# Three ordinary column pairs in place of four in each feed-forward of a one-core transformer step

## The chip, the cores and the metric

The kernel runs on one core of one Trainium2 chip. The metric is the device time of one execution in microseconds (us); the time of a version is the median of its runs. Engines are named as in the profile: PE is TensorE's matmul stream and PEld its weight loads, DVE is VectorE, ACT is ScalarE, POOL is GpSimd, and SP is the sync engine, which here only issues the DMAs of the large inputs. `L805` is line 805 of the kernel's file.

## What is computed

One layer of a hybrid backbone on 640 tokens (128 context and 512 latent) of width 1024, all in float32: a half-step SwiGLU feed-forward, a token mixer, and a second half-step feed-forward, each with RMS norms and with shift, scale and gate vectors from a modulation product. What matters here are the two feed-forwards and the modulation:

```python
def swiglu(h, w_in, w_out):
    g, u = jnp.split(h @ w_in, 2, axis=-1)
    return (jax.nn.silu(g) * u) @ w_out

mod = (jax.nn.silu(cond) @ w_mod + b_mod)[:, None, :]
sh1, sc1, g1, sh2, sc2, g2, sh3, sc3, g3 = jnp.split(mod, 9, axis=-1)
h = rms_norm(x, norm_pre[0]) * (1.0 + sc1) + sh1
x = x + 0.5 * g1 * rms_norm(swiglu(h, ffn_w_in[0], ffn_w_out[0]), norm_post[0])
```

`ffn_w_in` has 2 x 2816 columns, which are 22 pairs of a gate block and a value block of 128 columns each; `w_mod` has 9 x 1024 columns, loaded as 18 slabs of 512 columns (2 MB each).

## The kernel before, in words

**Precision.** Each float32 operand is split into a high and a low part of the fast matmul type, and a product is three matmuls: high by high, high by low, low by high. For a weight slab (1024 rows x 128 columns, 512 KB) SP loads the whole into the buffer of the low part (`load`, L411), ACT casts the high part (`next_hi`, L1198), POOL subtracts to get the low part (`subtract`, L534, and `low`, L544), and PE multiplies. Some slabs of later stages are subtracted by DVE (`LO_DVE`, L137).

**Stages.** `STAGES` (L48) lists the weight slabs of every stage with the ring of buffers through which they go, and `plan` (L85) works out from it which slab must be done before a buffer is loaded again (`FREE`). `FRESH` (L106) is the order in which ACT and POOL prepare ordinary slabs. The stages are `in0`, `in0s` (first feed-forward, input side), `out0A`, `out0B` (its output side, for the token tiles 0 to 2 and then 3 and 4), the mixer from `vuA` to `woB`, and `in1A`, `in1B`, `in1s`, `out1A`, `out1B`. In `in1A` and `in1B` the same ordinary slabs are used twice, for tokens 0 to 383 and for the rest, and stay in their buffers.

**Two kinds of column pair.** The first `EARLY_PAIRS` = 4 pairs of each feed-forward are ordinary: 2 slabs x 8 row blocks x 3 passes over all 640 tokens, 96 matmuls of 320 columns or as many columns in another cut. The other `SEVEN` = 18 pairs use a seven-product scheme on 2 x 2 quadrants (`seven_products`, L816): 7 products x 4 row blocks x 3 passes = 84 matmuls of 320 columns (`product`, L801). It needs combinations of the weights, made for each pair (`first_sums` L1910, `last_sum` L1926 and `lows` L1937 on DVE; `gate_highs` L1418 and `value_highs` L1424 on ACT; `seven_low` L552 on POOL), and combinations of the tokens, made once for a feed-forward (`token_combinations` L1892 on DVE, `token_highs` L1439 on ACT, `token_lows` L547 on POOL). Each product waits for its operands; the second product of the first pair also waits until the hidden tiles of the ordinary pairs have left PSUM (L833).

**Order in the first feed-forward.** After each ordinary slab named in `MOD_AFTER` (slabs 2, 3, 5 and 7) and after each of the first ten seven-product pairs, PE multiplies one modulation slab (`late_mod`, L874). SP's list (L459 to L486) puts the loads in one queue: slabs 4, 5 and 6, modulation slab 2, slab 7, and then for each seven-product pair its two slabs and one more modulation slab. A modulation slab waits until the one before it has been used (`next_mod`, L469). On DVE the weight sums and lows of the first seven-product pair come behind the hidden tile of ordinary pair 2 (L2032); on ACT its casts come in ordinary pairs 2 and 3 (L1486 to L1489).

**The output side.** `out_group` on PE (L723) runs 22 slabs for three token tiles in `out0A` (11 slabs for the first 512 output columns, 11 for the rest). Slab m of the first 11 needs hidden tiles 0 to 2m+1, split into high and low:

```python
            if grp == 0 and blk == 0:
                pe.wait_ge(sem(ready[0]), ready[1] + k + 2)
```

ACT makes the cast (`whole_high`, L1326) and DVE the subtraction (`whole_low`, L1963). The first `EARLY_PAIRS` + 2 casts come before the stage. The others are spread over it, two behind each slab and behind the weight casts that `after_slab` (L1205) releases there:

```python
                after_slab(i + m, 2 if grp else 1)
                ...
                    for j in range(EARLY_PAIRS + 2 * m + 2, min(FT, EARLY_PAIRS + 2 * m + 4)):
                        whole_high(b // 2, j)
```

SP loads slab m+4 when slab m is done, and puts the two DMAs of the gain rows ahead of slab 8 (`load_gains`, L436).

Of the kernel before, what the change touches and what calls it, by code (L numbers as in the profile page):

```python
# [26 lines left out]

GROUP = ((0, 1, 2), (3, 4))
G_COLS = ((0, 384), (384, 640))
EARLY_PAIRS = 4  # L30

# [4 lines left out]
SEVEN = FT - EARLY_PAIRS  # L38
# [7 lines left out]

KEEP = [6, 7, 8, 9, 10]
STAGES = [  # L48
    ("in0", 2 * EARLY_PAIRS, [0, 1, 2, 11, 0, 1, 2, 0], False),
    ("in0s", 2 * SEVEN, [12, 1, 2, 0], False),  # L50
    ("out0A", FT, [1, 2, 0, 3], False), ("out0B", FT, [0, 4, 5, 1, 2], False),
    ("vuA", 8, [6, 1, 7, 2, 8, 0, 9, 10], False), ("vuB", 8, [6, 1, 7, 2, 8, 0, 9, 10], True),
    ("heads", 4 * NH, [1, 2, 0], False),
    ("merge", 3 * KT, [2, 0, 1], False),
    ("woA", KT, KEEP[:3] + [2, 0, 1] + KEEP[3:], False),
    ("woB", KT, KEEP[:3] + [2, 0, 1] + KEEP[3:], True),
    ("in1A", 2 * EARLY_PAIRS, KEEP[:2] + [2, 0, 1] + KEEP[2:], False),
    ("in1B", 2 * EARLY_PAIRS, KEEP[:2] + [2, 0, 1] + KEEP[2:], True),
    ("in1s", 2 * SEVEN, [12, 2, 0, 1], False),
    ("out1A", FT, [2, 0, 1, 3], False), ("out1B", FT, [1, 4, 5, 2, 0], False),  # L60
]


MOD_ROUNDS = ((0, 2), (1, 3))
MOD_AFTER = [2, 3, 5, 7]
EARLY_GATES = 3
LAST = 3

# [16 lines left out]
def plan():  # L85
# [35 lines left out]
    branch = base["merge"] + MERGE.index(("br", 3))  # L121
    for n, after in ((0, branch), (1, branch), (2, branch), (6, base["woA"] - 1), (7, base["woA"] - 1)):
        free[base["woA"] + n] = after
    for n, after in ((0, base["woA"]), (1, base["woA"] + 1)) + tuple((n, base["in1A"] - 1) for n in (5, 6, 7)):
        free[base["in1A"] + n] = after
    free[base["in0s"]] = 4
    free[base["in1s"]] = base["in1A"] - 1
    return base, buf, free, order, need, fresh


def hybrid_step_kernel(nc, x_prompt, x_sample, state_hgrn, c, c_ctx, w_mod, b_mod, norm_pre, norm_post,
# [53 lines left out]
    def tile_at(n):  # L185
        return mid_at + n * TB
# [213 lines left out]
    def _(sp):  # L400
# [70 lines left out]
            sp.wait_ge(sem("mod_mm"), MOD_EARLY + (1 if i == 2 else i))  # L471
            load_mod(i)

        for n in (4, 5, 6):
            load_in0(n)
        next_mod(2)
        load_in0(7)
        for p in range(SEVEN):
            j = EARLY_PAIRS + p
            load(BASE["in0s"] + 2 * p, 0, KT, w0[:, :, j * P:(j + 1) * P])  # L480
            load(BASE["in0s"] + 2 * p + 1, 0, KT, w0[:, :, DFF + j * P:DFF + (j + 1) * P])
            if 3 + p < MOD_LATE:
                next_mod(3 + p)
        wo0 = ffn_w_out[0, 0].rearrange("(k p) n -> p k n", p=P)
        load_out(0, 0, wo0)
        load_out(0, 1, wo0)  # L486
# [46 lines left out]
    def _(pool):  # L533
# [35 lines left out]
        for n, i in enumerate(FRESH):  # L569
            if n < 3 or i in LO_DVE:  # L570
                continue
            if i in (6, BASE["out1A"]):
                token_lows(int(i != 6))
            if i in (BASE["out0A"], BASE["out1A"]):
                for p in range(SEVEN):
                    seven_low(int(i == BASE["out1A"]), p)
            step = 2 if BASE["heads"] <= i < BASE["merge"] + 2 * EARLY_GATES else 4
            pool.wait_ge(hi_done, n + 1)
            for k in range(0, KT, step):
                m = subtract(i, k, k + step)  # L580
            m.then_inc(lo_done, 1)
# [611 lines left out]
    def _(act):  # L1193
# [287 lines left out]
        for j in range(EARLY_PAIRS):  # L1481
            after_slab(2 * j)
            gate_out(j, (two(TT[0][:, :]), halves(2 if j == 1 else 0)))
            if j == 1:
                token_highs(0)
            if j == 2:  # L1486
                gate_highs(0, 0)
            if j == 3:
                value_highs(0, 0)  # L1489
            after_slab(2 * j + 1)  # L1490
        seven_gates(0)
# [181 lines left out]
        for stage, grp in (("in1A", 0), ("in1B", 1)):  # L1673
            c0, c1 = G_COLS[grp]
            for j in range(EARLY_PAIRS):
                n = (1 + grp) * EARLY_PAIRS + j
                after_slab(BASE[stage] + 2 * j)
                gate_out(n, (TT[0][:, c0:c1], bank(early_bank(grp, j, 0))[:, 0:c1 - c0]))
                if (grp, j) == (0, 0):
                    h_high_half(1, 4)  # L1680
                    h_hi(1, 4)
                if (grp, j) == (1, 0):
                    token_highs(1)
                if (grp, j) == (1, 1):
                    gate_highs(1, 0)
                if (grp, j) == (1, 2):
                    value_highs(1, 0)
        seven_gates(1)
        out_group(2, 0)
# [3 lines left out]
    def _(dve):  # L1693
# [332 lines left out]
        for j in range(EARLY_PAIRS):  # L2026
# [2 lines left out]
            V.tensor_tensor(two(M32[:, j, :]), two(TT[0][:, :]), halves(1), ALU.mult).then_inc(sem("hid_ready"), 1)  # L2029
            if j == 0:  # L2030
                token_combinations(0)
            if j == 2:  # L2032
                first_sums(0, 0)
                last_sum(0, 0)
                lows(0, 0)
# [327 lines left out]
```

## Time and profile before

| | us |
|---|---|
| runs | 1403.70, 1403.95, 1404.72 |
| median of the 3 runs | 1403.95 |
| the profiled execution's own time | 1403.82 |
| its span, first to last instruction | 1401.9 |
| PE busy in the span | 1380.4 (98%) |
| mean granted TensorE clock | 0.999 of full speed |

A timeline row gives the start in us from the span's start, the length in us, the engine, the line, the operation with output and inputs, the count of merged instructions, and in brackets the idle time before it with what ended it. Matmuls overlap in the pipeline: a matmul of 320 columns is shown with some 0.31 us, but the next one starts 0.147 us later. So lengths of PE work are taken from start to start. A DVE or POOL row begins when the engine takes the instruction up, so a row can hold a wait for a resource.

### The profile page before, as it was taken

The numbers are of one execution on the slowest core, as the hardware profiler recorded it, in microseconds if no ns is written. First come the engines' busy times: TensorE is split into PE (matmuls) and PEld (weight loads), VectorE is DVE, ScalarE is ACT, GpSimd is POOL, SyncE is SP. The second block draws the span as 40 slices with busy tenths as digits, with TensorE's granted clock in tenths as the row PEclk, the third lists the DMA queues.
The fourth block names the chain that finished last, engine by engine and source line by source line (L and its number), as shares of the span: only waits on it lengthen the run. The fifth ranks groups of instructions, "written<-read, shape, count | busy, mean of one in ns | idle before, by whom it ended". The sixth has DMA issues, their size and how long they took to land.

```text
span 1401.9 us, 23454 instructions
## 1 busy us (share of the span) xinstructions
PE 1380.4 (98%) x9561; PEld 1261.6 (90%) x9561; DVE 722.6 (52%) x1086; ACT 578.3 (41%) x933; POOL 716.1 (51%) x528
## 2 busy tenths in 40 slices
PE   6999999999999999999999999999999999999998
PEld 5799898999888888999999999988999999988886
DVE  5726565766712431478776312235567666676033
ACT  5233333444534663244445222257243443355243
POOL 1465545465865672324223433542466655668653
PEclk9999999999999999999999999999999999999999
DMA  9756676233535651212112222333122223334465
GB/s 347 258 156 221 216 234 210 61 92 90 173 127 166 194 174 49 61 54 62 53 41 65 76 76 76 106 105 105 32 75 84 81 78 91 91 104 153 135 195 181
DMA packets 215294, 173.34 MB, mean 124 GB/s; under 512 B 6472, under 2 KB 175636, under 8 KB 215060
## 3 DMA queue, kind: packets, MB, share of 16 engines
q1 hardware_dynamic: 212448, 170.61, 39.1%
q8 instruction: 76, 1.25, 0.4%
q10 hardware_dynamic: 2740, 1.24, 0.3%
q14 instruction: 30, 0.25, 0.1%
HBM read 168.65 MB, written 3.17 MB: 123 GB/s over the span
## 4 chain that ended last, share of the span: by engine, by line
PE 91%; DVE 2%; ACT 2%; DMA 1%; issue 1%; POOL 1%; SPq 1%; ACTq 0%; DVEq 0%; POOLq 0%
PE PP L805 31%; PE PP L603 27%; PE PP L622 9%; PE PP L624 9%; PE PP L623 9%; PE PP L661 2%; DMA W_in<-in_ffn_w_in 1%; PE PP L869 1%; PE PP L995 1%; PE PP L647 1%; POOL W_lo L536 1%; PE PP L1011 1%; DVE XTOK L1796 0%; ACT W_hi L1203 0%; ACT YB L1280 0%
## 5 line engine op out<-in xcount | busy, mean ns | idle before, releaser
L536 POOL TENSOR_TENSOR W_lo<-W_in,W_hi 128x512 fp32r<-128x512 f32 (+1 forms) x308 | 386.3, 1280 | 448.2 <-ACT W_hi L1203 440.8
L545 POOL TENSOR_TENSOR W_lo<-W_in,W_hi 128x512 fp32r<-128x512 f32 x108 | 169.6, 1584 | 190.4 <-ACT S_hi L1430 186.3
L1203 ACT ACTIVATE W_hi<-W_in 128x1024 fp32r<-128x1024 f32 x145 | 153.0, 1056 | 220.6 <-PE PP L624 116.3
L622 PE MATMUL PP<-W_hi,Mlo 128*128 128x512 f32 x440 | 172.5, 392 | 2.3 <-POOL W_lo L536 1.9
L624 PE MATMUL PP<-W_hi,Mhi 128*128 128x512 f32 x440 | 171.3, 389 | 0.0
L623 PE MATMUL PP<-W_lo,Mlo 128*128 128x512 f32 x440 | 171.3, 389 | 0.0
L603 PE MATMUL PP<-Hhi,W_hi 128*128 128x320 f32 (+2 forms) x640 | 154.1, 316 | 0.0
L603 PE MATMUL PP<-Hlo,W_hi 128*128 128x320 f32 (+2 forms) x640 | 149.6, 309 | 0.0
L603 PE MATMUL PP<-Hhi,W_lo 128*128 128x320 f32 (+2 forms) x640 | 149.6, 309 | 0.0
L805 PE MATMUL PP<-Hhi,W_hi 128*128 128x320 f32 x432 | 134.9, 312 | 0.5 <-DVE TT L1989 0.5
L805 PE MATMUL PP<-Hhi,W_lo 128*128 128x320 f32 x432 | 133.5, 309 | 0.0
L805 PE MATMUL PP<-Hlo,W_hi 128*128 128x320 f32 x432 | 133.4, 309 | 0.0
L603 PEld LDWEIGHTS PP<-Hhi,W_hi 128*128 128x128 f32 x640 | 106.6, 188 | 4.7 <-issue 3.5
L545 POOL TENSOR_TENSOR S_lo<-S_in,S_hi 128x512 fp32r<-128x512 f32 x72 | 108.1, 1502 | 3.4 <-ACT S_hi L1431 3.4
L603 PEld LDWEIGHTS PP<-Hlo,W_hi 128*128 128x128 f32 x640 | 108.1, 188 | 0.0
L603 PEld LDWEIGHTS PP<-Hhi,W_lo 128*128 128x128 f32 x640 | 108.0, 188 | 0.0
L622 PEld LDWEIGHTS PP<-W_hi,Mlo 128*128 128x128 f32 x440 | 82.6, 188 | 22.0 <-issue 2.3
L624 PEld LDWEIGHTS PP<-W_hi,Mhi 128*128 128x128 f32 x440 | 82.6, 188 | 17.4
L623 PEld LDWEIGHTS PP<-W_lo,Mlo 128*128 128x128 f32 x440 | 82.6, 188 | 16.9
L805 PEld LDWEIGHTS PP<-Hhi,W_hi 128*128 128x128 f32 x432 | 81.1, 188 | 10.0 <-issue 9.1
L805 PE MATMUL PP<-T_hi,S_hi 128*128 128x320 f32 x288 | 89.0, 309 | 0.0
L805 PE MATMUL PP<-T_lo,S_hi 128*128 128x320 f32 x288 | 89.0, 309 | 0.0
(280 smaller groups left out, 2966.3 us busy)
## 6 DMA issues: line engine op xcount, KB each, us to landing
W_in<-in_ffn_w_out SPq DMA_DIRECT2D x176, 256.0 KB, 3.3
W_in<-in_ffn_w_in SPq DMA_DIRECT2D x83, 512.0 KB, 4.5
modl<-in_w_mod SPq DMA_DIRECT2D x14, 2048.0 KB, 8.1
W_in<-in_w_in SPq DMA_DIRECT2D x32, 512.0 KB, 3.8
modw<-in_w_mod SPq DMA_DIRECT2D x4, 2048.0 KB, 14.1
HL<-g_rows SPq DMA_DIRECT2D x6, 512.0 KB, 6.2
V_in<-in_w_in SPq DMA_DIRECT2D x10, 256.0 KB, 4.1
O_in<-in_w_out SPq DMA_DIRECT2D x10, 256.0 KB, 6.2
```

Of the source, the lines that this page charges most:

```text
L536: return nc.gpsimd.tensor_tensor(lo[:, k0:k1, :], full[:, k0:k1, :], hi[:, k0:k1, :].bitcast(fp32), ALU.subtract)
L545: return nc.gpsimd.tensor_tensor(lo, full, hi.bitcast(fp32), ALU.subtract)
L603: m = mm(out[:, 0:c1 - c0], w[:, k, :], src[:, c0:c1], start=lead and n == 0 and a == 0, stop=tail and n == len(x) - 1 and a == 2)
L622: mm(out, xh, wh, start=lead and kk == 0, stop=False)
L623: mm(out, xh, wl, start=False, stop=False)
L624: m = mm(out, xl, wh, start=False, stop=tail and kk == 1)
L647: return nc.tensor.transpose(out, in_, ident[0:k, 0:k])
L661: m = mm(PP[3][32 * q:32 * q + 32, 0, :], S2[:, k, 30 - 2 * i:62 - 2 * i], w[:, k, :], start=first and k < 4, stop=k >= 4, skip_group_chec ...
L805: m = mm(out, wk[:, k, :], xk[:, k, :], start=not add and k == 0 and a == 0, stop=k == KH - 1 and a == 2, skip_group_check=add)
L869: m = mm(PP[n][:, half, 0:HALF], w[:, k, :], src[:, half * HALF:(half + 1) * HALF], start=k == 0 and a == 0, stop=k == KT - 1 and a == 2)
L995: m = mm(near(pair_of(hd, lev))[32 * q:32 * q + 32, ch, :], KX[lev % 2][:, at:at + 32], queries, start=True, stop=True)
L1203: A(W[i][0], W[i][2], ACT.Copy).then_inc(hi_done, 1)
```

## The change

`EARLY_PAIRS` becomes 3, so that each feed-forward has 3 ordinary and 19 seven-product pairs, and what depends on it is moved:

- Slabs 6 and 7 of `in0` and the last two of `in1A` and `in1B` are dropped. `MOD_AFTER` becomes slabs 2, 3 and 5, so modulation slab 3 is multiplied behind the first seven-product pair.
- SP: the value slab of the first seven-product pair is loaded behind modulation slab 2. Then SP waits until modulation slab 1 has been used and loads its gate slab. From then on a pair's two slabs come ahead of the modulation slab that used to come one pair earlier.
- DVE: the weight sums and lows of the first seven-product pair move from behind ordinary pair 2 to behind pair 1. In the second feed-forward `token_combinations` moves ahead of the hidden tile of pair 2, and the weight sums move behind the first hidden tile of `in1B`.
- ACT: `value_highs` of the first seven-product pair directly follows `gate_highs`. POOL: in the first feed-forward `token_lows` now follows all ordinary slabs.
- Buffers 0, 1 and 2 are renamed in all later stages. In `in1s` the first pair gets the buffers 12 and 9, which are free as soon as `in1A` begins.

```diff
-EARLY_PAIRS = 4
+EARLY_PAIRS = 3
...
-    ("in0", 2 * EARLY_PAIRS, [0, 1, 2, 11, 0, 1, 2, 0], False),
-    ("in0s", 2 * SEVEN, [12, 1, 2, 0], False),
-    ("out0A", FT, [1, 2, 0, 3], False), ("out0B", FT, [0, 4, 5, 1, 2], False),
+    ("in0", 2 * EARLY_PAIRS, [0, 1, 2, 11, 0, 1], False),
+    ("in0s", 2 * SEVEN, [12, 2, 0, 1], False),
+    ("out0A", FT, [0, 1, 2, 3], False), ("out0B", FT, [2, 4, 5, 0, 1], False),
...
-    ("in1A", 2 * EARLY_PAIRS, KEEP[:2] + [2, 0, 1] + KEEP[2:], False),
-    ("in1B", 2 * EARLY_PAIRS, KEEP[:2] + [2, 0, 1] + KEEP[2:], True),
-    ("in1s", 2 * SEVEN, [12, 2, 0, 1], False),
-    ("out1A", FT, [2, 0, 1, 3], False), ("out1B", FT, [1, 4, 5, 2, 0], False),
+    ("in1A", 2 * EARLY_PAIRS, KEEP[:2] + [1, 2, 0] + KEEP[2:3], False),
+    ("in1B", 2 * EARLY_PAIRS, KEEP[:2] + [1, 2, 0] + KEEP[2:3], True),
+    ("in1s", 2 * SEVEN, [12, 9] + [1, 2, 0, 12] * SEVEN, False),
+    ("out1A", FT, [1, 2, 0, 3], False), ("out1B", FT, [0, 4, 5, 1, 2], False),
...
-MOD_AFTER = [2, 3, 5, 7]
+MOD_AFTER = [2, 3, 5]
...
-        for n in (4, 5, 6):
+        for n in (4, 5):
             load_in0(n)
         next_mod(2)
-        load_in0(7)
-        for p in range(SEVEN):
+        j = EARLY_PAIRS
+        load(BASE["in0s"] + 1, 0, KT, w0[:, :, DFF + j * P:DFF + (j + 1) * P])
+
+        sp.wait_ge(sem("mod_mm"), MOD_EARLY + 2)
+        load(BASE["in0s"], 0, KT, w0[:, :, j * P:(j + 1) * P])
+        for p in range(1, SEVEN):
             j = EARLY_PAIRS + p
-            load(BASE["in0s"] + 2 * p, 0, KT, w0[:, :, j * P:(j + 1) * P])
-            load(BASE["in0s"] + 2 * p + 1, 0, KT, w0[:, :, DFF + j * P:DFF + (j + 1) * P])
-            if 3 + p < MOD_LATE:
-                next_mod(3 + p)
+            load_pair(BASE["in0s"] + 2 * p, w0, j)
+            if 2 + p < MOD_LATE:
+                next_mod(2 + p)
...
             if j == 2:
                 gate_highs(0, 0)
-            if j == 3:
                 value_highs(0, 0)
...
             if j == 0:
                 token_combinations(0)
-            if j == 2:
+            if j == 1:
                 first_sums(0, 0)
                 last_sum(0, 0)
                 lows(0, 0)
...
         early_hidden(0, 1)
+        token_combinations(1)
         early_hidden(0, 2)
-        token_combinations(1)
-        early_hidden(0, 3)
         early_hidden(1, 0)
-        early_hidden(1, 1)
         first_sums(1, 0)
         last_sum(1, 0)
+        early_hidden(1, 1)
+        lows(1, 0)
         early_hidden(1, 2)
-        lows(1, 0)
-        early_hidden(1, 3)
         seven_sums(1)
```

## Rows read from the trace of the kernel before

**Rows 1.** The page, part 1: busy time of each engine over the span.
```profile
PE 1380.4 (98%) x9561; PEld 1261.6 (90%) x9561; DVE 722.6 (52%) x1086; ACT 578.3 (41%) x933; POOL 716.1 (51%) x528
```

**Rows 2.** Waits of PE: total us, times, longest us.
```profile
PE PP L622 <- POOL W_lo L536: 1.9, 3, 0.7
```

**Rows 3.** Timeline of PE, end of the ordinary pairs, first feed-forward.
```profile
83.04 1.92 PE L661 MATMUL PP<-modl,S 128*32 128x512 f32 x16
...
99.16 1.92 PE L661 MATMUL PP<-modl,S 128*32 128x512 f32 x16
101.02 0.42 PE L805 MATMUL PP<-Hhi,W_hi 128*128 128x320 f32 x1
```

**Rows 4.** Timeline of DVE: the same sum of two neighbouring seven-product pairs.
```profile
299.53 0.49 DVE L1989 TENSOR_TENSOR TT<-TT,PP 128x320 f32<-128x320 f32 x1 [3.09 <-PE PP L805]
...
311.85 0.49 DVE L1989 TENSOR_TENSOR TT<-TT,PP 128x320 f32<-128x320 f32 x1 [3.09 <-PE PP L805]
```

**Rows 5.** Timeline of PE, ordinary pairs of the second feed-forward.
```profile
966.26 0.33 PE L603 MATMUL PP<-Hhi,I_hi 128*128 128x384 f32 x1
...
974.61 1.04 PE L647 MATMUL PP<-ident,YB 128*128 128x128 f32 x8
...
1000.47 0.28 PE L603 MATMUL PP<-Hhi,I_hi 128*128 128x256 f32 x1
...
1023.50 0.31 PE L805 MATMUL PP<-Hhi,W_hi 128*128 128x320 f32 x1
```

**Rows 6.** Timeline of PE in `out0A`: slabs 0, 7 and 8 begin.
```profile
345.85 0.47 PE L622 MATMUL PP<-W_hi,Mlo 128*128 128x512 f32 x1 [0.66 <-POOL W_lo L536]
...
374.69 0.39 PE L622 MATMUL PP<-W_hi,Mlo 128*128 128x512 f32 x1
...
378.94 0.50 PE L622 MATMUL PP<-W_hi,Mlo 128*128 128x512 f32 x1
```

**Rows 7.** The page, part 6: DMAs, KB each, median us from issue to landing.
```profile
W_in<-in_ffn_w_in SPq DMA_DIRECT2D x83, 512.0 KB, 4.5
modl<-in_w_mod SPq DMA_DIRECT2D x14, 2048.0 KB, 8.1
```

**Rows 8.** Timeline of POOL: token lows and first pair's lows, first feed-forward.
```profile
72.52 8.83 POOL L545 TENSOR_TENSOR T_lo<-T_in,T_hi 128x1280 fp32r<-128x1280 f32 x3 [7.19 <-ACT T_hi L1442]
...
94.05 1.36 POOL L545 TENSOR_TENSOR S_lo<-S_in,S_hi 128x512 fp32r<-128x512 f32 x1 [3.43 <-ACT S_hi L1431]
```

**Rows 9.** Timelines of POOL and DVE in `in1B`: a DVE sum beside POOL's token lows.
```profile
1006.92 8.80 POOL L545 TENSOR_TENSOR T_lo<-T_in,T_hi 128x1280 fp32r<-128x1280 f32 x3 [15.06 <-ACT T_hi L1442]
...
1013.06 3.21 DVE L1919 TENSOR_TENSOR S_in<-W_in 128x512 f32<-128x512 f32 x1 [0.45 <-DMA W_in<-in_ffn_w_in]
1016.30 0.69 DVE L1923 TENSOR_TENSOR S_in<-S_in,W_in 128x512 f32<-128x512 f32 x1
```

**Rows 10.** Timelines of DVE and ACT: token combinations of the second feed-forward.
```profile
992.82 1.48 DVE L1890 TENSOR_TENSOR BSUM<-Hhi,Hlo 128x1280 f32<-128x1280 f32 x1
...
1003.25 1.49 DVE L1908 TENSOR_TENSOR T_in<-T_in,BSUM 128x1280 f32<-128x1280 f32 x1
...
1005.58 3.58 ACT L1442 ACTIVATE T_hi<-T_in 128x1280 fp32r<-128x1280 f32 x3
```

**Rows 11.** Timelines of SP, ACT and DVE in `out0A`.
```profile
367.83 32.17 SPq L423 DMA_DIRECT2D W_in<-in_ffn_w_out  x17
...
373.93 1.06 ACT L1203 ACTIVATE W_hi<-W_in 128x1024 fp32r<-128x1024 f32 x1 [4.37 <-DMA W_in<-in_ffn_w_out]
374.89 1.35 ACT L1335 ACTIVATE Mlo<-M 128x640 fp32r<-128x640 f32 x2
...
375.65 10.56 DVE L1965 TENSOR_TENSOR Mhi<-M,Mlo 128x640 fp32r<-128x640 f32 x6 [3.28 <-ACT Mlo L1335]
```

**Rows 12.** Timelines of PE and DVE in `out1A`.
```profile
1274.90 0.39 PE L622 MATMUL PP<-W_hi,Mlo 128*128 128x512 f32 x1
...
1274.91 10.58 DVE L1965 TENSOR_TENSOR Mhi<-M,Mlo 128x640 fp32r<-128x640 f32 x6 [1.48 <-ACT Mlo L1335]
```

More of the change, by code:

```diff
@@ L48 @@
 STAGES = [
-    ("in0", 2 * EARLY_PAIRS, [0, 1, 2, 11, 0, 1, 2, 0], False),
-    ("in0s", 2 * SEVEN, [12, 1, 2, 0], False),
-    ("out0A", FT, [1, 2, 0, 3], False), ("out0B", FT, [0, 4, 5, 1, 2], False),
[L52 to L56, printed above, removed]
-    ("in1A", 2 * EARLY_PAIRS, KEEP[:2] + [2, 0, 1] + KEEP[2:], False),
-    ("in1B", 2 * EARLY_PAIRS, KEEP[:2] + [2, 0, 1] + KEEP[2:], True),
-    ("in1s", 2 * SEVEN, [12, 2, 0, 1], False),
-    ("out1A", FT, [2, 0, 1, 3], False), ("out1B", FT, [1, 4, 5, 2, 0], False),
+    ("in0", 2 * EARLY_PAIRS, [0, 1, 2, 11, 0, 1], False),
+    ("in0s", 2 * SEVEN, [12, 2, 0, 1], False),
+    ("out0A", FT, [0, 1, 2, 3], False), ("out0B", FT, [2, 4, 5, 0, 1], False),
+    ("vuA", 8, [6, 0, 7, 1, 8, 2, 9, 10], False), ("vuB", 8, [6, 0, 7, 1, 8, 2, 9, 10], True),
+    ("heads", 4 * NH, [0, 1, 2], False),
+    ("merge", 3 * KT, [1, 2, 0], False),
+    ("woA", KT, KEEP[:3] + [1, 2, 0] + KEEP[3:], False),
+    ("woB", KT, KEEP[:3] + [1, 2, 0] + KEEP[3:], True),
+    ("in1A", 2 * EARLY_PAIRS, KEEP[:2] + [1, 2, 0] + KEEP[2:3], False),
+    ("in1B", 2 * EARLY_PAIRS, KEEP[:2] + [1, 2, 0] + KEEP[2:3], True),
+    ("in1s", 2 * SEVEN, [12, 9] + [1, 2, 0, 12] * SEVEN, False),
+    ("out1A", FT, [1, 2, 0, 3], False), ("out1B", FT, [0, 4, 5, 1, 2], False),
 ]
 MOD_ROUNDS = ((0, 2), (1, 3))
-MOD_AFTER = [2, 3, 5, 7]
+MOD_AFTER = [2, 3, 5]
 EARLY_GATES = 3
@@ L123, in plan @@
         free[base["woA"] + n] = after
-    for n, after in ((0, base["woA"]), (1, base["woA"] + 1)) + tuple((n, base["in1A"] - 1) for n in (5, 6, 7)):
+    for n, after in ((0, base["woA"]), (1, base["woA"] + 1)) + ((5, base["in1A"] - 1),):
         free[base["in1A"] + n] = after
-    free[base["in0s"]] = 4
+    free[base["in0s"]] = 3
     free[base["in1s"]] = base["in1A"] - 1
+    free[base["in1s"] + 1] = base["in1A"] - 1
     return base, buf, free, order, need, fresh
@@ L206, in hybrid_step_kernel @@
     EXTRA = slab_buffer("W11", tile_at(14) - 8192)
+    KEPT["in1s"] = KEPT["in1A"]
     KEPT.update({"vuB": KEPT["vuA"], "woB": KEPT["woA"], "in1B": KEPT["in1A"]})
@@ L571, in _ @@
                 continue
-            if i in (6, BASE["out1A"]):
-                token_lows(int(i != 6))
+            if i in (BASE["out0A"], BASE["out1A"]):
+                token_lows(int(i == BASE["out1A"]))
             if i in (BASE["out0A"], BASE["out1A"]):
@@ L1685, in _ @@
                     gate_highs(1, 0)
-                if (grp, j) == (1, 2):
                     value_highs(1, 0)
```

## The prediction

> **What bounds the kernel now.** I read the page's busy line first, then the waits of PE, then timelines. The busy line shows PE at 1380.4 of 1401.9 us [rows 1]: PE is the bound from its first matmul to the end. The waits show why PE work counts in full: the weight lows hold PE up three times, for 1.9 us in all [rows 2]. So a matmul taken away shortens the run, unless something that was just in time is now late. The timelines must show how much time each preparation had in hand. The profiled execution took 1403.82 us, 1.9 more than its span, and 0.13 less than the median of 1403.95; the sum is made on 1403.82 and 0.13 is added. About 0.2% (2.8 us) is what a measurement here can tell from no change: 1401.1 to 1406.8.
>
> **PE work.** Lengths go from start to start. In the first feed-forward a modulation slab takes 101.02 - 99.16 = 1.86, so slabs 6 and 7 ran from 83.04 + 1.86 = 84.90 to 99.16: 14.26 us [rows 3]. A seven-product pair takes 311.85 - 299.53 = 12.32 [rows 4], which is 84 matmuls of 0.147. Gain 1.94. Modulation slab 3 is multiplied one pair later; it costs its 1.86 there too. In the second feed-forward two slabs of `in1A` take 974.61 - 966.26 = 8.35, and two of `in1B` a quarter of 1023.50 - 1000.47 = 23.03, that is 5.76: 14.11 in all [rows 5], gain 1.79. Together **-3.73**.
>
> **First slab of the output stages.** PE stood 0.66 before slab 0 of `out0A` [rows 6], waiting for POOL's low of that slab; `out1A` shows the same. With 19 pairs the buffer of slab 0 belonged to the gate slab of the last pair but one, and the rule in `after_slab` lets ACT cast it one pair earlier, POOL then being idle. The wait goes in both stages: **-1.32**. Next in line is hidden tile 3, needed only by slab 1, 4.1 later.
>
> **Front of the first seven-product pair, first feed-forward.** PE could start it at 84.90, not 101.02. Its weights: the gate slab is loaded when modulation slab 1 is used, at about 83.04 - 14.26 = 68.8, and lands 4.5 later [rows 7], near 73.3; what waits behind this new wait in SP's queue are the slabs of pair 1 and modulation slab 3. That slab is issued at 84.9, lands after 8.1 [rows 7] and is wanted after the pair, near 97: covered by 4 us. Pair 1 is wanted by DVE only after its second product. The preparation is not covered. POOL's three token lows start at 72.52 and take 8.83 [rows 8], as they did, since ACT's casts are where they were. But DVE's four weight sums, which stood behind them, are now beside them, and the rows show what this does: a sum of 0.69 took 3.21 us, and ended 0.55 after the run of POOL (1006.92 + 8.80 = 1015.72) [rows 9]. So the two engines take turns, a whole instruction each. By the Trainium skill, "SBUF — State Buffer", section "Who interferes with whom", a `tensor_tensor` with both inputs in SBUF contends with GpSimd's reads, and the second to issue fully blocks; these rows agree.
>
> Taking turns: lows and four sums end at 72.52 + 8.83 + 4 x 0.55 = 83.55. POOL's first weight low (1.3, from 1.36 [rows 8]) ends at 84.9, just when PE wants it. Then DVE's first low, POOL's, DVE's second (0.55, 1.3, 0.55) end at 87.3. Only behind them stands, in DVE's order, the hidden tile of pair 2 (0.85, from 0.69 for 512 columns), done at 88.15, and the second product waits for it (L833). It was wanted at 84.90 + 1.76 = 86.66. With row lengths in place of hold times (0.69, 1.36) it is 89.1. Late by 1.5 to 2.4: I take **+1.7**, near the hold times, as these are what the shared run shows. Ends: 0 (DVE gets through early) and 1.7 + 2.9 (one more token low in the way).
>
> **Front in the second feed-forward.** `in1B` starts at 1000.47 - 8.35 = 992.12 and three quarters of 23.03 put the first product at 1009.39. The token combinations, 11.9 us from 992.82 to 1004.74 [rows 10], now start behind hidden tile 1, near 984.6 (`in1A`'s first four slabs and 0.8 of transposes from 966.26, and the tile), and end near 996.5. The cast followed 0.84 behind them and POOL 1.34 behind the cast (1006.92 - 1005.58) [rows 9, 10]: POOL starts at 998.7. The chain moved up 8.2 us and PE 14.1; before, the first low had five us in hand, now it has none. POOL's 8.80, four sums of 0.55 in turn, and 1.3 end at 1011.0; the first product is late by 1.6, and T3's low, in turn with POOL, by some 0.3 more: **+1.9**, ends 0 and 4.8.
>
> **Supply of hidden tiles on the output side.** Slab m needs tiles 0 to 2m+1. Before, 6 casts came ahead of the stage and tile 2m+1 was cast behind slab m-3. With `EARLY_PAIRS` 3 only 5 come ahead, the loop shifts by one, and tile 2m+1 is cast behind slab m-2: one slab (28.84 / 7 = 4.12 us [rows 6]) of notice is gone. The diff does not touch this loop. Where ACT is prompt the rest is just enough: behind a slab come one weight cast (1.06), one tile cast (0.68) and a low (10.56 / 6 = 1.76 in a run beside POOL) [rows 11], 3.5 of 4.1 us. At two slabs it isn't. Behind slab 0 of `out0A` ACT casts two weights, which makes 4.6: late by **+0.55** (ends 0 and 1.3); in `out1A` one of the two is free earlier. And behind slab 5 ACT first casts the weights of slab 8, which were issued at 367.83, behind the gain rows in SP's queue; it waited 4.37 us and cast them at 373.93, and the tile cast came at 374.89 [rows 11]. That cast is now the one for tile 15. Its low starts at 375.65; as the first of its run it waits for one POOL instruction at most and is done after some 1.45, a little under the run's 1.76, at 377.1. PE wants slab 7 at 374.69 [rows 6]: **+2.5** (ends 0, if the weights come sooner, and 2.8). The 0.13 that slab 8 lost (378.94 - 374.69 = 4.25 against 4.12 [rows 6]) is then inside that wait: -0.13. In `out1A` the same low starts at 1274.91 and slab 7 is wanted at 1274.90 [rows 12]: 1.45 and a semaphore, **+1.5** (ends 0 and 1.8).
>
> A load's price has a rule: by the Trainium skill, "SBUF — State Buffer", section "The DMA setup-cost knee", a DMA takes about 2 us plus its bytes at 436 GB/s, by estimate 3.2 us for slab 8's 512 KB. By that the cast would stand 2.9 earlier and slab 7 would wait for nothing. The row's 6.1 us from issue to cast, behind the gain rows, decides, and the sum keeps 2.5.
>
> **Without cost.** The renamed buffers keep the order in which each is freed. In `in1s` the buffers 12 and 9 are free when `in1A` starts, 30 us before DVE reads them. The later `late_mod`, `fold_mod` and gain steps stand six pairs from the end, as before.
>
> **Sum.** First feed-forward -1.94 - 0.66 + 1.7 + 0.55 + 2.5 - 0.13 = +2.02; second -1.79 - 0.66 + 1.9 + 1.5 = +0.95. 1403.82 + 2.97 + 0.13 = **1406.9**: the work saved is more than given back in waits at four places.
>
> **Rivals.** *All covered*: DVE's sums pass ahead of POOL and the tiles come in time. Then -3.73 - 1.32 - 0.13 = -5.2: **1398.7**, faster. For it: PE hardly waits now. Against it: each of the four margins is negative in the rows. Chance 0.08. *Only the fronts are late*: the weights of slab 8 land sooner and the tile casts keep pace. Then -5.2 + 3.6 = -1.6: **1402.3**, no change. It decides from the point where slab 8's cast stands before 371.5 in the old times. By the Trainium skill's rule on a DMA's setup cost, above, this is the case. Against it: `out1A` shows the same late run. Chance 0.12. *Only the output side is late*: POOL and DVE overlap in the fronts, so that hidden tile 2 ends before 86.66 and the second feed-forward's first low before 1009.3. Then -5.2 + 4.55 = -0.65: **1403.3**. Against it: the 3.21 us row. Chance 0.14. *The lows fall behind for good*: two POOL and two DVE subtractions in turn take 4.0 of each slab's 4.1 us, so any slip makes several slabs wait, for 3 us more: **1410**. For it: runs of 10.56 us without a gap. Chance 0.12. The forecast has 0.54.
>
> **How the numbers follow.** Within the forecast the ends of the six terms give 1404.5 to 1409.5, a little over half of it above 1406.8. Slower by over 0.2%: 0.31 + 0.12 = 0.43. Faster: 0.08 and a quarter of the 0.12, 0.11. No change: 0.46. The range leaves out the fastest case and the tail of the slowest: 1400.5 to 1409.5. The likeliest case's own range is 1404.5 to 1409.5.
>
> **What would show it.** Seven-product pairs start 16 us earlier and PE's matmul count falls by 24. PE shows a wait on DVE before the second product of the first pair, on POOL before the first of the second feed-forward, on DVE's `Mhi` before slab 7 of `out0A` (about 2.5 us) and of `out1A` (1.5), and none on POOL at slab 0. It is wrong if those waits are absent or if PE waits at a modulation slab.

## The result: slower by 0.2%, and the profile after

The changed kernel took 1408.4 us in the median of 11 runs (1405.13 to 1410.11), beside 1404.34 us for the kernel before in 11 runs. The medians differ by 4.06 us; the ratio on record is 1.0022 with an interval of 1.0013 to 1.0031. The forecast was 1406.9 us, slower, with a range of 1400.5 to 1409.5. The profiled execution is the longest of the 11: 1410.11 us with a span of 1408.0, so it can show more stops than most runs have. The runs lie 5 us apart, and that is itself something to explain. Among the experiments one run of 1934.71 us, at a granted clock of 0.66, stands apart from all others; it is not explained and is left out of the ratio.

The page's header and its busy line, of the kernel after; they answer to [rows 1].

```profile
span 1408.0 us, 23471 instructions
...
PE 1380.1 (98%) x9537; PEld 1260.2 (89%) x9537; DVE 755.4 (54%) x1109; ACT 582.6 (41%) x946; POOL 721.8 (51%) x530
```

PE has the 24 matmuls less that were forecast (9561 to 9537), and yet its busy time fell by 0.3 us only. DVE is busy 33 us more for 23 more instructions; part of that is instructions that wait inside their own time, as the timelines below show.

The waits of PE, of the kernel after (total us, times, longest us); they answer to [rows 2].

```profile
PE PP L627 <- DVE Mhi L1968: 3.4, 4, 2.1
PE PP L652 <- ACT YB L1292: 2.2, 1, 2.2
...
PE PP L810 <- POOL W_lo L550: 0.8, 1, 0.8
PE PP L810 <- DVE M L2032: 0.8, 1, 0.8
PE PP L627 <- POOL W_lo L541: 0.7, 1, 0.7
```

Of the three waits of 0.7 us for POOL's low of a slab, one is left: the two at slab 0 of `out0A` and `out1A` are gone, as forecast. In their place stand the tile lows (`Mhi`), the two fronts (POOL's `W_lo` of L550 and DVE's `M`, 0.8 each), and a wait of 2.2 us for `YB`, a token tile, that was not forecast. Below, a *stop* of PE is what a step from one matmul's start to the next has over the usual 0.23 us (0.15 for 320 columns); it is some 0.15 longer than the wait beside it.

**Front of the first feed-forward.** Timelines of POOL, DVE and PE, kernel after; they answer to [rows 3, 8].

```profile
73.00 9.75 POOL L550 TENSOR_TENSOR T_lo<-T_in,T_hi 128x1280 fp32r<-128x1280 f32 x3 [7.19 <-ACT T_hi L1447]
83.38 1.68 POOL L550 TENSOR_TENSOR W_lo<-W_in,W_hi 128x512 fp32r<-128x512 f32 x1 [0.63 <-DVE W_in L1927]
...
73.15 3.37 DVE L1922 TENSOR_TENSOR S_in<-W_in 128x512 f32<-128x512 f32 x1 [0.80 <-DMA W_in<-in_ffn_w_in]
76.56 3.35 DVE L1926 TENSOR_TENSOR S_in<-S_in,W_in 128x512 f32<-128x512 f32 x1
79.83 3.46 DVE L1927 TENSOR_TENSOR W_in<-W_in 128x512 f32<-128x512 f32 x1
83.22 0.68 DVE L1937 TENSOR_TENSOR S_in<-W_in,S_in 128x512 f32<-128x512 f32 x1
...
87.23 0.81 DVE L2032 TENSOR_TENSOR M<-TT,PP 128x640 f32<-128x640 f32 x1
...
88.19 0.38 PE L810 MATMUL PP<-T_hi,S_hi 128*128 128x320 f32 x1 [0.81 <-DVE M L2032]
```

A sum of 0.68 us takes 3.4 when a token low stands in front of it: three sums, three token lows, one after the other. ([rows 9] showed only one sum held up by one token low; the prediction read the turns into it, and here they are.) POOL's first weight low ends at 85.06, in time for the pair's first product at 85.35. The hidden tile behind the two DVE lows ends at 88.04, and the second product stops PE for 0.97 us.

**Front of the second feed-forward.** Timelines of POOL and PE, kernel after; they answer to [rows 9].

```profile
1005.12 10.08 POOL L550 TENSOR_TENSOR T_lo<-T_in,T_hi 128x1280 fp32r<-128x1280 f32 x3 [13.97 <-ACT T_hi L1447]
1015.16 1.72 POOL L550 TENSOR_TENSOR W_lo<-W_in,W_hi 128x512 fp32r<-128x512 f32 x1
...
1016.93 0.41 PE L810 MATMUL PP<-Hhi,W_hi 128*128 128x320 f32 x1 [0.85 <-POOL W_lo L550]
```

The first weight low ends at 1016.88, behind all three token lows, and PE stops for 1.00 us ahead of the first product.

**Tiles in `out0A` and `out1A`.** Timelines of SP, ACT, DVE and PE, kernel after; they answer to [rows 6, 11, 12].

```profile
364.33 1.99 SPq L446 DMA_DIRECT2D YB<-in_t_mask  x1
366.37 17.01 SPq L425 DMA_DIRECT2D W_in<-in_ffn_w_out  x8
...
373.27 1.06 ACT L1208 ACTIVATE W_hi<-W_in 128x1024 fp32r<-128x1024 f32 x1 [4.76 <-DMA W_in<-in_ffn_w_out]
374.24 1.35 ACT L1340 ACTIVATE Mlo<-M 128x640 fp32r<-128x640 f32 x2
...
374.99 6.85 DVE L1968 TENSOR_TENSOR Mhi<-M,Mlo 128x640 fp32r<-128x640 f32 x4 [3.76 <-ACT Mlo L1340]
...
376.42 0.50 PE L627 MATMUL PP<-W_hi,Mlo 128*128 128x512 f32 x1 [2.12 <-DVE Mhi L1968]
...
378.42 0.63 PE L627 MATMUL PP<-W_hi,Mlo 128*128 128x512 f32 x1
378.85 0.63 PE L628 MATMUL PP<-W_lo,Mlo 128*128 128x512 f32 x1
...
381.10 0.39 PE L628 MATMUL PP<-W_lo,Mlo 128*128 128x512 f32 x1
...
1276.50 0.50 PE L627 MATMUL PP<-W_hi,Mlo 128*128 128x512 f32 x1 [0.71 <-DVE Mhi L1968]
...
1281.07 0.50 PE L627 MATMUL PP<-W_hi,Mlo 128*128 128x512 f32 x1 [0.20 <-DVE Mhi L1968]
```

The chain is the one that was forecast: the weights of slab 8 (two loads of 256 KB) are issued at 366.37 behind the gain rows and the mask table, which SP loads in the kernel before too, ACT casts them at 373.27, tile 15 only then, and PE stops at slab 7 for 2.29 us. In `out1A` PE stops for 0.88 us at slab 6 (1276.50), one slab earlier than forecast, and for 0.36 us at slab 7 (1281.07). What follows the stop in `out0A` was not forecast: from some 1.2 us after the stop the matmuls start 0.43 us apart instead of 0.23, until 380.9. The table by stretches shows why (columns: the engines' busy time and counts, then the granted clock, DMA share, GB/s).

```profile
376.40:381.00 4.60, 4.58 (x13) 3.63 (x14) 4.60 (x3) 1.39 (x3) 4.60 (x3) 0.63 0.19 71
381.00:390.00 9.00, 9.00 (x42) 7.42 (x41) 5.26 (x4) 4.00 (x5) 5.06 (x5) 1.00 0.38 118
```

The granted clock is 0.63 in the stretch and 1.00 behind it: most of the stretch ran at the lower level, 1.2 in place of 2.4 GHz. From 376.42 to 380.87 there are 12 matmul steps, 4.45 us. Behind a like stop without a low clock (the pause alone, below) the same 12 steps took 2.89 us: the low clock costs some **1.6 us** on top of the stop.

**Beginning of the mixer.** Timelines of DVE, POOL and PE and the table by stretches, of the kernel after; the first two lines are those of DVE and POOL of the kernel before at the same place.

```profile
504.81 2.35 DVE L1789 TENSOR_TENSOR ST<-ST 128x1 f32<-128x1 f32 x2
...
504.62 2.53 POOL L536 TENSOR_TENSOR W_lo<-W_in,W_hi 128x512 fp32r<-128x512 f32 x2
```

```profile
508.49 9.66 DVE L1792 TENSOR_TENSOR ST<-ST 128x1 f32<-128x1 f32 x2
...
508.04 2.55 POOL L541 TENSOR_TENSOR W_lo<-W_in,W_hi 128x512 fp32r<-128x512 f32 x2
...
515.54 2.52 POOL L541 TENSOR_TENSOR V_lo<-V_in,V_hi 128x512 fp32r<-128x512 f32 x2
...
522.68 1.09 PE L652 MATMUL PP<-ident,YB 128*128 128x128 f32 x8 [2.24 <-ACT YB L1292]
...
520.00:528.00 8.00, 5.76 (x23) 4.39 (x23) 2.82 (x7) 7.17 (x12) 2.53 (x2) 0.79 0.01 2
```

Two additions of one number per partition took 9.66 us. They ended when POOL, which worked without a gap from 497.91 on (most rows are left out above), ran out of work at 518.06: here DVE did not get its turn between POOL's instructions. In the kernel before POOL worked without a gap too, and DVE got its turn within 2.35 us; so the unbroken work of POOL allows the stop but does not force it. The token tile that hangs on the sums came late, PE stopped for 2.40 us, and matmuls 0.43 us apart followed from 524.07 to 527.7, for another 1.6 us at the lower level (the mean granted clock is 0.79 from 520 to 528). The change does not touch this place. So the questions for the experiments were: which of these stops make up the difference, whether the slab 7 stop comes from the notice of the tiles or from the weights of slab 8, and whether the mixer's stop is chance, in both kernels.

### The profile page after: what moved, and what is told of

It is laid out like the page before. It is cut to its first block, busy times and chain, and to the rows that moved or that the text cites. A ratio compares the mean times of both kernels' runs of the same rounds, so it can differ in the third digit from the quotient of the medians.

```text
span 1408.0 us, 23471 instructions
## 1 busy us (share of the span) xinstructions
PE 1380.1 (98%) x9537; PEld 1260.2 (89%) x9537; DVE 755.4 (54%) x1109; ACT 582.6 (41%) x946; POOL 721.8 (51%) x530
## 3 DMA queue, kind: packets, MB, share of 16 engines
q10 hardware_dynamic: 2740, 1.24, 0.3%
## 4 chain that ended last, share of the span: by engine, by line
PE 88%; DVE 4%; DMA 3%; ACT 1%; issue 1%; SPq 1%; POOL 1%; DVEq 0%; ACTq 0%; POOLq 0%
PE PP L810 33%; PE PP L608 22%; PE PP L627 8%; PE PP L629 8%; PE PP L628 8%; PE PP L666 2%; DMA W_in<-in_ffn_w_in 1%; PE PP L874 1%; DMA W_in<-in_ffn_w_out 1%; PE PP L652 1%; PE PP L1000 1%; DVE ST L1792 1%; PE PP L1016 1%; POOL T_lo L550 0%; SPq L425 0%
## 5 line engine op out<-in xcount | busy, mean ns | idle before, releaser
L541 POOL TENSOR_TENSOR W_lo<-W_in,W_hi 128x512 fp32r<-128x512 f32 (+1 forms) x304 | 377.0, 1266 | 455.0 <-ACT W_hi L1208 447.5
L550 POOL TENSOR_TENSOR W_lo<-W_in,W_hi 128x512 fp32r<-128x512 f32 x112 | 176.3, 1588 | 185.2 <-ACT S_hi L1435 182.1
L608 PE MATMUL PP<-Hhi,W_hi 128*128 128x320 f32 (+2 forms) x608 | 146.7, 316 | 0.0
L810 PE MATMUL PP<-Hhi,W_hi 128*128 128x320 f32 x452 | 141.3, 313 | 1.3 <-POOL W_lo L550 0.8
L608 PE MATMUL PP<-Hlo,W_hi 128*128 128x320 f32 (+2 forms) x608 | 142.3, 309 | 0.0
L608 PE MATMUL PP<-Hhi,W_lo 128*128 128x320 f32 (+2 forms) x608 | 142.3, 309 | 0.0
L810 PE MATMUL PP<-Hhi,W_lo 128*128 128x320 f32 x452 | 139.7, 309 | 0.0
L810 PE MATMUL PP<-Hlo,W_hi 128*128 128x320 f32 x452 | 139.6, 309 | 0.0
L550 POOL TENSOR_TENSOR S_lo<-S_in,S_hi 128x512 fp32r<-128x512 f32 x76 | 116.3, 1531 | 0.0
L810 PE MATMUL PP<-T_hi,S_lo 128*128 128x320 f32 x304 | 93.9, 309 | 0.0
```

The costliest lines, as they stand in the source:

```text
L541: return nc.gpsimd.tensor_tensor(lo[:, k0:k1, :], full[:, k0:k1, :], hi[:, k0:k1, :].bitcast(fp32), ALU.subtract)
L550: return nc.gpsimd.tensor_tensor(lo, full, hi.bitcast(fp32), ALU.subtract)
L608: m = mm(out[:, 0:c1 - c0], w[:, k, :], src[:, c0:c1], start=lead and n == 0 and a == 0, stop=tail and n == len(x) - 1 and a == 2)
L810: m = mm(out, wk[:, k, :], xk[:, k, :], start=not add and k == 0 and a == 0, stop=k == KH - 1 and a == 2, skip_group_check=add)
```

## Experiments

Unless it says otherwise a kernel is the changed one with the edit shown. The first four ran on one chip, where the kernel before took 1404.41 us (35 runs, 1403.22 to 1408.81); the next four on one where it took 1405.24 (26 runs, 1403.36 to 1410.06); the last on one where it took 1404.61.

### The tiles as early as before

```diff
-            for j in range(EARLY_PAIRS, EARLY_PAIRS + 2):
+            for j in range(EARLY_PAIRS, EARLY_PAIRS + 3):
                 whole_high(f, j)
...
-                    for j in range(EARLY_PAIRS + 2 * m + 2, min(FT, EARLY_PAIRS + 2 * m + 4)):
+                    for j in range(EARLY_PAIRS + 2 * m + 3, min(FT, EARLY_PAIRS + 2 * m + 5)):
```

> The change with one part undone: ScalarE again casts the tiles of the hidden layer as far ahead of the output slabs as before (tiles 3, 4 and 5 behind the last gate; behind the weight casts of slab m of the group tiles 6+2m and 7+2m, where the change had 5+2m and 6+2m). Theory (the notice of the tiles is what the change gave away): the PE waits for VectorE's tile parts go in out0A (0.54 us at slab 2, 2.3 us at slab 7) and the two of out1A (0.9 and 0.4 us), and with the 2.3 us stop also the stretch at half clock behind it (13 matmuls of slab 7 in 4.45 us instead of 2.95, 1.5 us): about 5 us less than the changed kernel on this chip, median about 1403.5 us. Rival 1 (the same casts now hold the weights): a wait for a weight part at slabs 2 to 4 takes their place, less than 2 us gained. Rival 2 (the low clock at slab 7 has its own cause): the waits go, the low clock stays, 4 us gained.

Measured: 1401.76 us in the median of 12 runs, 0.9984 [0.9972, 0.9997] of the kernel before. Seven runs lie between 1401.18 and 1401.76, one at 1402.76, three between 1405.49 and 1407.16; the twelfth is the run of 1934.71. The profiled execution is one of the upper ones (1406.84) and shows what they consist of, first in the waits of PE, then in the timelines of DVE and PE:

```profile
PE PP L652 <- ACT YB L1292: 2.2, 1, 2.2
PE PP L627 <- DVE Mhi L1968: 1.9, 1, 1.9
```

```profile
507.73 9.81 DVE L1792 TENSOR_TENSOR ST<-ST 128x1 f32<-128x1 f32 x2
...
379.61 0.50 PE L627 MATMUL PP<-W_hi,Mlo 128*128 128x512 f32 x1 [1.90 <-DVE Mhi L1968]
```

The stops at slab 7 and both of `out1A` are gone, and the one at slab 2 is down from 0.54 to 0.18 us. The stop of 2.05 us at 379.61 is one at slab 8, whose own tiles now wait behind its late weights (cast at 374.63 here), with a granted clock of 0.61 behind it; and the mixer's stop is back. What follows: the median is 6.6 us under the changed kernel's, more than the 5 expected. In the trace of the change the stops that this edit removes, with the low clock behind slab 7, add up to some 5.5 us; what the other 1.1 us are was not traced. So the tiles' notice is the main part of what the change lost; and the delay of slab 8's weights is a cause of its own that can strike at slab 7 or at slab 8.

### The order at the two beginnings

In `lows`, between DVE's two weight lows of the first pair; the loop over the ordinary pairs ends one earlier; and in POOL's `token_lows`, ahead of the third token low of the second feed-forward:

```diff
+            if (f, p) == (0, 0):
+                dve.wait_ge(slab_done, 2 * EARLY_PAIRS)
+                dve.wait_ge(sem("gate_ready"), EARLY_PAIRS)
+                V.tensor_tensor(two(M32[:, EARLY_PAIRS - 1, :]), two(TT[0][:, :]), halves(1), ALU.mult)\
+                    .then_inc(sem("hid_ready"), 1)
...
-        for j in range(EARLY_PAIRS):
+        for j in range(EARLY_PAIRS - 1):
...
+                if f and n == 2:
+                    first_low(f, 0)
```

> The change with the order at the two beginnings of the seven-product pairs changed: in the first feed-forward VectorE makes the third hidden tile between the two weight parts instead of behind both; in the second POOL makes the first weight part ahead of the third token part. Theory (each wait is a matter of order in one queue): the 0.97 us before the second product of the first feed-forward and the 1.0 us before the first product of the second go, 2.0 us less than the changed kernel, about 1406.4 us. Rival (the engines there are full, so that the next operand is late by as much): the waits move to the second or third product of the same pair and the time stays at 1408.4 us within 0.5 us.

Measured: 1405.97 us (12 runs, 1404.4 to 1409.94), 1.0008 [0.9998, 1.0018]. Its timeline of PE has no stop in the first feed-forward's first pair, and in the second one only this, at the pair's fourth product:

```profile
1016.97 0.42 PE L817 MATMUL PP<-Hhi,I_hi 128*128 128x320 f32 x1 [0.40 <-POOL I_lo L550]
```

So in this execution the first front is a pure matter of order, 0.97 us. The second gives 1.00 and takes 0.56 back at the next low that is just in time: POOL works there from 1007.66 to 1020.33 without a gap. By the trace 1.4 us of the 2.0 expected.

### The 128x1 sums with one tensor input

```diff
-            V.tensor_tensor(ST[:, 2, t:t + 1], ST[:, 0, t:t + 1], ST[:, 1, t:t + 1], ALU.add)\
+            V.tensor_scalar(ST[:, 2, t:t + 1], ST[:, 0, t:t + 1], ST[:, 1, t:t + 1], None, ALU.add)\
```

> The change with VectorE's 128x1 sum of the two square sums (9.66 us for two of them ahead of the mixer's first products, while POOL worked without a gap) written as an addition of a per-partition scalar, so that only one of its inputs is a tensor. Theory (an addition of two tensors in SBUF must wait for POOL to pause, and how long is chance): the two sums take under 1 us, the PE wait of 2.2 us at 522 us and the half clock behind it are gone, 4 us less in the executions that had it; median about 1405.5 us and the runs closer together (within 2 us instead of 5). Rival 1 (the scalar takes the same way into VectorE): nothing changes, sums of 2 to 10 us, median 1408.4 us, runs 5 us apart. Rival 2 (the spread of the runs comes from another place): the sums are short, the runs still lie 4 to 5 us apart.

Measured: 1407.79 us (12 runs, 1405.79 to 1411.52), no gain. The timeline of DVE:

```profile
509.21 0.32 DVE L1792 TENSOR_SCALAR ST<-ST 128x1 f32<-128x1 f32 x2
...
511.55 8.58 DVE L1799 SCALAR_TENSOR_TENSOR XTOK<-YB,ST,XTOK 128x1024 f32<-128x1024 f32 x1
```

Right on the instruction and wrong on the place: the rewritten sums take 0.32 us beside the same POOL, but the next instruction with two tensors in SBUF, `x_add`, takes 8.58 instead of 1.28, and PE stops for 1.72 us all the same. The signs of the second rival came (short sums, runs 5.7 us apart), but that the hold moves to the next instruction was in none of the three. By the Trainium skill, "SBUF — State Buffer", section "Who interferes with whom", it is the second tensor read that meets GpSimd's reads; the 0.32 and the 8.58 agree.

> The kernel before with the same rewritten 128x1 sum and nothing else. It tells whether the same chance lies behind the two bands of the kernel before (1403.7 to 1404.7 us and 1406.9 to 1408.7 us). Theory: the upper band goes, all runs within 1403 to 1405 us. Rival (the upper band has another cause): runs at 1406.5 us and above stay, one in three.

Measured: 1404.88 us (12 runs, 1403.15 to 1406.37). No run above 1406.5, as the theory had it, but six of the twelve lie above its 1405, and there are no two bands. The median is higher than expected. After the finding above this edit could not decide the question.

### The gain rows spread out

```diff
-                if grp == 0 and m == (4 if b == 1 else 8):
-                    load_gains(b)
+                if grp == 0 and b == 0 and 8 <= m < 11:
+                    load_gains(b, (m - 8,))
+                elif grp == 0 and b and m == (4 if b == 1 else 8):
+                    load_gains(b, (0, 1))
```

> The change with the two loads of the gain rows (512 KB each) and the mask table (448 KB), which SyncE issues in one go ahead of slab 8 of out0A, spread out: one each ahead of slabs 8, 9 and 10. The tiles are cast as late as in the change. Theory (the 2.3 us stop at slab 7 is a tile that waits on ScalarE behind the weights of slab 8, and these wait behind the 1.5 MB): slab 8's weights are cast about 3 us earlier, the stop at slab 7 and the half clock behind it go, 3.8 us less than the changed kernel, median about 1404.6 us; the 0.54 us at slab 2 stay. Rival (VectorE beside POOL makes the tile parts too slowly, whatever the weights do): a stop of over 1 us at slab 7 stays, less than 1.5 us gained.

Measured: 1405.03 us (12 runs, 1402.79 to 1408.59), 0.9999 [0.9987, 1.001]: 3.4 us under the changed kernel's median (the kernel before took 1404.34 us beside that one and 1405.24 beside this). The profiled execution is the lowest run. Its timelines of SP and ACT, then the wait of PE for tiles:

```profile
362.90 0.45 SPq L446 DMA_DIRECT2D HL<-g_rows  x1
365.95 0.82 SPq L425 DMA_DIRECT2D W_in<-in_ffn_w_out  x2
366.87 0.38 SPq L446 DMA_DIRECT2D HL<-g_rows  x1
...
370.65 1.06 ACT L1212 ACTIVATE W_hi<-W_in 128x1024 fp32r<-128x1024 f32 x1 [2.17 <-DMA W_in<-in_ffn_w_out]
```

```profile
PE PP L631 <- DVE Mhi L1972: 1.8, 3, 0.7
```

Slab 8's weights, issued at 365.95, are cast at 370.65, 4.7 us later and not 6.9 (366.37 to 373.27), and in this execution PE no longer stops at slab 7; the granted clock has no fall there. The three waits left are slab 2 (0.38) and two of `out1A` (0.68 and 0.75, where the change had 0.71 and 0.20). So with the tiles cast late, the weights of slab 8 decide the stop, as the forecast had it. By the Trainium skill, "SBUF — State Buffer", section "The DMA setup-cost knee", the slab's 512 KB as one load would take 3.2 us by estimate; 4.7 us with one gain row of 512 KB issued ahead and one behind, and 6.9 behind both and the mask table, show how far weights that share the queue, here in two loads of 256 KB, are from that.

### Repairs together, without and with a pause of POOL

The first kernel has the three repairs above (tiles, beginnings, gain rows); the second adds:

```diff
+            if i == BASE["vuA"] + 3:
+                pool.wait_ge(sem("x_new"), NCH)
             step = 2 if BASE["heads"] <= i < BASE["merge"] + 2 * EARLY_GATES else 4
             pool.wait_ge(hi_done, n + 1)
```

> The change with three repairs together: the tiles cast as early as before, the order at the beginnings of the seven-product pairs, the gain rows spread out. Theory (the stops are separate and add): the lower end of the runs with the tiles repaired, 1401.2 us, less 1.4 us of the two beginnings: most runs at 1399.8 us; runs 4 to 5 us above it remain, from VectorE waiting for POOL at the beginning of the mixer. Rival (POOL and VectorE share what is gained at one place and lose it at the next): 1401 us or more for most runs.

> As the kernel with the three repairs, and POOL waits ahead of the fourth weight part of the mixer's first stage until VectorE has added the last two token tiles of the first feed-forward. Theory (there POOL works without a gap, any VectorE instruction with two inputs in SBUF can be held up to the end of POOL's work, and the weight part has 3 us to spare): the sums and additions take under 4 us in every run, the runs 4 to 5 us above the others are gone, median 1399.8 us and all within 2 us. Rival 1 (the pause makes a weight part late): a wait for POOL of 1 us or more in the mixer's first stage, median above 1401 us. Rival 2 (the upper runs have another cause): they stay.

Measured without the pause: 1401.79 us (8 runs, 1399.58 to 1405.47), 0.997 [0.9957, 0.9983]. With it: **1399.66 us** (5 runs, 1399.41 to 1400.14), 0.9957 [0.9942, 0.9971], the best of all kernels here. The lowest run of the first is where it was expected, but five of the eight lie at 1401 us or more, which was the rival's number. Its mechanism was not: the trace (1402.09) shows the mixer's stop again, 2.41 us, and with the pause it is gone. The timeline of DVE without the pause, and those of POOL and DVE with it:

```profile
503.16 9.67 DVE L1803 TENSOR_TENSOR ST<-ST 128x1 f32<-128x1 f32 x2
```

```profile
499.93 2.54 POOL L545 TENSOR_TENSOR V_lo<-V_in,V_hi 128x512 fp32r<-128x512 f32 x2
507.72 2.54 POOL L545 TENSOR_TENSOR W_lo<-W_in,W_hi 128x512 fp32r<-128x512 f32 x2 [5.25 <-DVE XTOK L1812]
...
502.62 0.22 DVE L1805 TENSOR_TENSOR ST<-ST 128x1 f32<-128x1 f32 x2
504.96 1.28 DVE L1812 SCALAR_TENSOR_TENSOR XTOK<-YB,ST,XTOK 128x1024 f32<-128x1024 f32 x1
...
506.36 1.28 DVE L1812 SCALAR_TENSOR_TENSOR XTOK<-YB,ST,XTOK 128x1024 f32<-128x1024 f32 x1
```

POOL stands still for 5.25 us and no slab of the mixer is late. The sums take 0.22 us and the additions 1.28 each, and the runs lie 0.73 us apart where they lay 5.9. So the stop at the mixer needs POOL's unbroken work; of the two edits tried against it only the break gave DVE a sure turn.

### The kernel before, with the two repairs that are not the change's

The kernel before with the gain rows spread out and the pause.

> The kernel before (four ordinary pairs) with the two repairs that do not belong to the change: gain rows spread out, and POOL's wait at the beginning of the mixer. It tells what the exchange of a pair is worth when both kernels are without chance stops. Theory: 1403.4 us, all runs within 2 us, no runs at 1406.5 us and above; so that three pairs with everything repaired stand 3.6 us below four pairs, of 5.05 us of PE work and first slabs gained. Rival (the kernel before gains as much from the repairs): 1401 us or less, the exchange is worth nothing.

Measured: 1403.65 us (11 runs, 1402.25 to 1404.11), 0.998 [0.9969, 0.9991]. All runs lie within 1.9 us; the runs above 1406, 12 of the 26 of the kernel before beside them, are gone here too. So that kernel had a chance stop of its own; no trace of such a run was taken, and the edit has two parts, so that it is the mixer's stop is likely and not shown. With everything repaired on both sides, three ordinary pairs take 1399.66 and four 1403.65: the exchange of a pair is worth 4.0 us, of the 5.05 forecast for PE work and first slabs.

### The pause alone

> The change with nothing but POOL's wait at the beginning of the mixer (until VectorE has added the last two token tiles). It tells how much of the changed kernel's median is chance at that place and how much is the change's own stops. Worked out from the traces: the profiled execution of the change lost there 2.6 us to the stop and 1.5 us to the half clock behind it; a share of the executions had it. Theory: no stop there any more, the runs that lay highest come down, median 1406.5 us and none above 1408.5 us; what is left above the 1399.7 us of the repaired kernel are the stops of the tiles (5.8 us) and of the two beginnings (1.4 us). Rival (the upper runs come from the stop at slab 7 alone, which differs from run to run): the median stays at 1408 us or above.

Measured: 1406.89 us (11 runs, 1404.56 to 1407.97), 1.0011 [1.0002, 1.0021]. The median is 1.5 us lower and no run is above 1408. The profiled execution is the lowest run, and it is telling: it has the stop in `out0A` without the low clock. The timeline of PE, then the table by stretches:

```profile
376.12 0.50 PE L629 MATMUL PP<-W_hi,Mlo 128*128 128x512 f32 x1 [1.78 <-DVE Mhi L1970]
```

```profile
376.00:381.00 5.00, 4.88 (x21) 4.04 (x22) 5.00 (x4) 1.92 (x4) 4.87 (x3) 1.00 0.25 83
```

A stop of 1.95 us, a granted clock of 1.00, 21 matmuls in 5 us. Without the mixer's stop and without a low clock the change can run in 1404.56 us. It is one execution: the other ten took 1405.18 to 1407.97, and one low clock of 1.6 us does not reach the upper of these. The stops themselves differ from execution to execution (slab 7: 1.95 us here, 2.29 in the change, 3.16 with the rewritten sums, where `out1A` stopped for 1.73 more); what the slower runs here consist of was not traced.

## Why the prediction was right, and by which of its steps

The direction held, and so did the mechanism: a stop at each of the places named, but for one slab in `out1A`. That the forecast (1406.9) came so near the median is in part luck, because two errors went against each other.

- **PE work, -3.73.** The 24 matmuls are gone, and the kernels with all repairs stand 4.0 us apart where this step and the next promised 5.05. Of the difference 0.75 is the stops that the repaired kernel still shows (0.56 in the second front, 0.19 at slab 2); 0.3 stays open.
- **First slab, -1.32.** Right: both waits of 0.66 are gone [rows 2, 6].
- **Front of the first feed-forward, +1.7.** Measured 0.97. The order of the turns was right, and they were a little shorter than forecast. The whole of this execution runs some 0.47 us later than the one before (PE 83.50 against 83.04 at the last modulation slab there, POOL's token lows 73.00 against 72.52), so the hidden tile's end at 88.04 stands at 87.57 in the old times, 0.6 before the forecast 88.15.
- **Front of the second feed-forward, +1.9.** Measured 1.00. POOL's token lows and the weight low took 11.76 us, where the step had put 12.3, and PE shows no wait for T3's low.
- **Tiles, +0.55, +2.5, -0.13, +1.5.** Measured 0.54 at slab 2, 2.29 at slab 7, no wait at slab 8, and 0.88 + 0.36 = 1.24 in `out1A`, the larger part at slab 6, where the step had no wait. The gain rows ahead of slab 8's weights were named as the cause, and the spread-out rows took the stop away.
- **What failed: the sum of stops was taken for the whole loss.** The six terms as measured give -5.05 + 0.97 + 1.00 + 0.54 + 2.29 - 0.13 + 1.24 = +0.86, not +2.97, that is 1404.7 on the profiled execution's 1403.82; the lowest run with the pause, without the low clock, took 1404.56. Missing are the half clock behind the stop at slab 7, 1.6 us when it comes, and the stop at the mixer, 2.4 us and 1.6 more when the clock falls there. Neither has a term in the prediction. With both the sum is +6.5, beside +6.29 between the two profiled executions; stretches without a stop of their own differ by up to 0.7.
- **The range.** The prediction says that the ends of its terms give 1404.5 to 1409.5, but does not work it out. Added up all one way they give some 1399 to 1414, so the range inside which the result fell was a judgement.
- **"Without cost".** The renamed buffers and the earlier load of the pair's weights show no wait of their own in any trace; they were not undone alone.
- **The rivals.** *All covered* priced -5.2, 1398.7; with the stops taken away by edits the kernel took 1399.66, 0.75 of the 1.0 between them in stops that it still has; so the price was about right and its condition was not met by the change alone. *Only the fronts are late* named slab 8's cast before 371.5 as its point; with the rows spread out the cast came at 370.65, about 371.5 in the old times (slab 2 began at 353.36 there and at 354.26 before), and the stop at slab 7 was gone: the rival's mechanism was right, but the change alone did not meet its condition. *Only the output side is late* did not come: both fronts stopped PE, for 0.97 and 1.00 us. *The lows fall behind for good* did not come: in the kernel after the slabs of `out0A` behind slab 7 wait for nothing.

With the pause alone the changed kernel still lies 2.3 us above the kernel before (1406.89 beside 1404.61), so that part of the difference does not come from the mixer. Why the clock fell behind some stops and not others stays open.

## What to carry to other kernels

When work is taken from the engine that bounds, list every queue that fed it with the notice it now has left: a loop whose bounds hang on the changed constant (here the tile casts) can lose a whole slab of notice without a line of it in the diff, and two constants there were worth most of 6.6 us. Two engines that hold each other up (here DVE's instructions with two tensor inputs in SBUF and POOL's lows) should be given a point at which one waits for the other, where the waiting one has time to spare; a wait of 5.25 us that made no slab late took nearly all the spread away (0.73 us in five runs). Large tables ahead of a tight load should be spread out.

## What the runs showed of the hardware that was not expected

- **Turns between DVE and POOL are not sure.** At 73 us of the kernel after a DVE instruction got in behind each one of POOL's. At the mixer, with POOL at work without a gap in every one of these executions, two additions of 128x1 took 9.66, 9.81 and 9.67 us in three of them (the change, the tiles, the three repairs), up to POOL's last instruction, and 2.35, 2.37 and 2.35 in three others (the kernel before, the order at the beginnings, the gain rows). What decides is not seen in these traces; the form with one tensor input and a per-partition scalar took 0.32 for two.
- **The granted clock can fall behind a stop of two microseconds.** In `out0A` the stops of 2.05 (the tiles), 2.25 (the order at the beginnings), 2.29 (the change) and 3.16 us (the rewritten sums) were followed by a mean granted clock of 0.61 to 0.66 over the next 4.4 to 5 us, the one of 1.95 (the pause) by 1.00. At the mixer 2.40 us was followed by the lower level in one execution (the change), 2.41 us in two others (the tiles, the three repairs) by 1.00. So the length of the stop alone does not say it.
